# Inverses of the delta rule among the last projections, scans among the steps of attention

## What is computed

```python
mod = jax.nn.silu(c) @ lp['w_mod'] + lp['b_mod']           # 24 pieces of 256 columns, for x and for ctx
h = _rms(x, lp['norm1']) * (1 + sc1) + sh1                 # 512 tokens; hc: 256 context tokens alike
z = h @ lp['w_in']                                         # f, aq, ak, av, dqkv, dz, gates
dqkv = jax.nn.silu(_dwconv(dqkv, lp['conv_w']))            # then l2 norm of q and k
# delta rule, per direction, chunk of 64 and head:
tmat = triangular_solve(eye + lmat, eye)                   # "inverse"
def step(S, inp):                                          # "scan", chunk after chunk
    v_new = u_i - w_i @ S
    o = (q_i * exp(g_i)) @ S + qk_i @ v_new
    S = S * exp(g_last) + (k_i * exp(g_last - g_i)).T @ v_new
# attention of 8 heads in 4 blocks of 128 queries over 768 keys
p = softmax(q @ k.T * scale);  o = p @ v
cat = concatenate([fourier(f), o_att, rms(o_dn) * silu(dz)])
x = x + g1 * (cat @ w_out)
```

## Time and profile before

| | us |
|---|---|
| median of three runs | 3356.98 |
| the profiled execution | 3348.67 |
| its span | 3346.8 |
| TensorE busy in the span | 3172.3 (95%) |
| VectorE busy | 1792.9 (54%) |
| ScalarE busy | 1110.7 (33%) |
| GpSimd busy | 65.1 (2%) |

### The profile page before, as it was taken

How to read it: one execution, slowest core, us unless ns; L and a number is a source line. 1 busy time by engine, 2 the same in 40 slices (tenths; PEclk the granted TensorE clock), 3 DMA queues, 4 the chain that set the end, 5 groups by cost and what they waited for, 6 DMA issues and landing times.

```text
span 3346.8 us, 42586 instructions
## 1 busy us (share of the span) xinstructions
PE 3172.3 (95%) x17664; PEld 2506.3 (75%) x17664; DVE 1792.9 (54%) x2536; ACT 1110.7 (33%) x1566; POOL 65.1 (2%) x95
## 2 busy tenths in 40 slices
PE   6886879989999999999999999999999999999997
PEld 3654774578888888876688888888887767888886
DVE  4444565353435434487865434654345877643446
ACT  3331115342323223324443222432224244432233
POOL 0000320000000000000000000000000000000000
PEclk8887998999999999999999999999999999999999
DMA  6231000023322232321122322233222212222222
GB/s 240 82 118 64 4 32 1 26 76 101 96 94 100 96 100 92 96 94 50 62 96 99 96 95 92 96 109 96 99 87 91 91 45 84 93 101 95 95 91 73
DMA packets 81935, 288.18 MB, mean 86 GB/s; under 512 B 9552, under 2 KB 11344, under 8 KB 81360
## 3 DMA queue, kind: packets, MB, share of 16 engines
q1 hardware_dynamic: 81744, 285.46, 25.3%
HBM read 283.33 MB, written 2.10 MB: 85 GB/s over the span
## 4 chain that ended last, share of the span: by engine, by line
PE 85%; DVE 4%; issue 2%; ACT 1%; DMA 1%; POOL 0%; DVEq 0%; ACTq 0%; POOLq 0%
PE PS L1308 74%; PE PS L1390 2%; PE PS L1616 1%; PE PS L1560 1%; PE PS L1580 1%; PE PS L1618 1%; PE PS L1568 1%; PE PS L1637 1%; PE PS L1626 1%; DMA MW<-in_w_mod 1%; DVE SM L2239 0%; PE PS L1599 0%; PE PS L1350 0%; ACT SPL L1667 0%; DVE GC L2407 0%
## 5 line engine op out<-in xcount | busy, mean ns | idle before, releaser
L1308 PE MATMUL PS<-HS,SPL 128*128 128x512 f32 (+1 forms) x7752 | 1802.3, 393 | 10.0 <-DVE HS L1991 7.3
L1308 PEld LDWEIGHTS PS<-HS,SPL 128*128 128x128 f32 (+1 forms) x7752 | 1454.9, 188 | 328.7 <-issue 20.0
L1943 DVE TENSOR_TENSOR SPL<-RAW,SPL 128x1024 fp32r<-128x1024 f32 (+1 forms) x491 | 584.1, 1193 | 722.4 <-ACT SPL L1667 718.8
L1667 ACT ACTIVATE SPL<-RAW 128x1024 fp32r<-128x1024 f32 (+1 forms) x491 | 502.9, 1028 | 871.0 <-PE PS L1308 870.7
L1308 PE MATMUL PS<-FF,SPL 128*128 128x512 f32 x2880 | 654.6, 390 | 0.0
L1308 PEld LDWEIGHTS PS<-FF,SPL 128*128 128x128 f32 x2880 | 541.0, 188 | 111.8
L2324 DVE SCALAR_TENSOR_TENSOR CA<-AP__150,CW,CA 128x512 f32<-128x512 f32 x240 | 180.1, 750 | 6.2
L1844 ACT ACTIVATE FF<-TMP 128x512 fp32r<-128x512 f32 x88 | 55.7, 633 | 235.1 <-DVE TMP L2294 235.1
L1838 ACT ACTIVATE SA<-SA 128x512 f32<-128x512 f32 x88 | 55.5, 633 | 191.7 <-DVE SA L2284 191.7
L2284 DVE TENSOR_TENSOR SA<-PS,R 128x512 f32<-128x512 f32 x88 | 60.5, 691 | 98.8 <-PE PS L1308 98.5
L2239 DVE TENSOR_REDUCE SM<-PS 128x1 f32<-128x768 f32 (+2 forms) x96 | 61.8, 644 | 82.5 <-PE PS L1561 45.1
(11 more groups left out here) (290 smaller groups left out, 2309.9 us busy)
## 6 DMA issues: line engine op xcount, KB each, us to landing
RAW<-in_w_ff_in SPq DMA_DIRECT2D x176, 512.0 KB, 3.6
RAW<-in_w_in SPq DMA_DIRECT2D x88, 512.0 KB, 3.6
RAW<-in_w_ff_out SPq DMA_DIRECT2D x80, 512.0 KB, 3.5
RAW<-in_w_ff SPq DMA_DIRECT2D x64, 512.0 KB, 3.6
MW<-in_w_mod SPq DMA_DIRECT2D x48, 512.0 KB, 4.8
RAW<-in_w_out SPq DMA_DIRECT2D x24, 512.0 KB, 3.6
RAW<-in_w_ple_gate SPq DMA_DIRECT2D x16, 512.0 KB, 3.6
RAW<-in_w_ff_out SPq DMA_DIRECT2D x16, 256.0 KB, 2.6
```

Of the source, the lines that this page charges most:

```text
L1308: m = pe.matmul(o, w[x][:, k, rows], r.T[:, r.k0 + k, y, 0:r.cols], start=r.start and k == 0 and (x, y) == (0, 0), stop=r.stop and k == r. ...
L1667: a.activation(SPL[:, s, 0, 0:n], RAW[:, s, 0:n], AF.Copy).then_inc(w_hi, 1)
L1943: v.tensor_tensor(SPL[:, s, 1, 0:n], RAW[:, s, 0:n], SPL[:, s, 0, 0:n], ALU.subtract).then_inc(w_lo, 1)
```

## The change

- Stage 1: `modulate` of a pair is written after the products of the next pair, the first split stands ahead of the third pair, and SyncE asks for the first four weight pieces right behind the first eight modulation pieces.
- Stage 2: `mods_apart` gives one modulation piece at every second call of `passed` in place of four at a time. The two blocks of a `conv3` run together (`together`, two buffers `CV2`).
- The inverses are put in a list `streams` and start when keys and values are there. During the last three projections `fine` cuts a weight piece in portions of two k-tiles (6 matmuls), and after each `tick` advances the streams by 2 x `pace` steps. The projections have banks 0 to 3, the streams and norms 4 to 7. The product for `PQK` is a step of its own (`inv_pq`).
- The scans are in `streams` as well; in attention each `tick` advances three streams, twice or three times in a step u. The streams have banks 6 and 7 there.
- Attention: steps go through four blocks of queries of two heads at once; `att_values` takes 128 queries of two heads every second step (128 columns in place of 512), its result goes to `AQ`, and `att_split` writes the parts at the end. The product by the reciprocal moves from VectorE to ScalarE.
- Tiles have new places. The inverses' tiles lie over `XT`, so x is loaded again (2 MB) ahead of the residual. `RT2` is gone, `RT` is kept and loaded early.

```diff
     behind, aside, soon, rate = [], [], [], [1]
+    streams, pace, fine = [], [0], [8]
...
+            for _ in range(pace[0]):
+                if streams:
+                    x = streams.pop(0)
+                    if next(x, None) is not None:
+                        streams.append(x)
 
...
+    apart, n_passed = [], [0]
+
     def passed():
+        n_passed[0] += 1
+        if apart and n_passed[0] % 2 == 0 and next(apart[0], None) is None:
+            apart.pop()
...
+                    for at in range(0, n, fine[0]):
+                        r = Rec()
+                        r.p, r.T, r.cols, r.use, r.i, r.k0, r.at, r.ncol = p, T, cols, us[i], i, a + at, at, ncol
+                        r.n = min(fine[0], n - at)
+                        r.opens, r.start = x == 0 and i == 0 and at == 0, a + at == 0
+                        r.stop = a + at + r.n == nk
...
+    def mods_apart(js):
+        for j in js:
+            while not room(1):
+                yield 1
+            u = single()
+            for a in range(0, 8, 4):
+                r = Rec()
+                r.p, r.use, r.k0 = mod_piece(W["w_mod"][j][:, a:a + 4, :]), u, a
+                r.used = u.mark if a else count(w_used)
+                emit("mod_mm", r)
+                if a:
+                    mod_rows(j, u)
+                yield 1
...
+    for k in range(5):
         if k == 2:
             emit("split_first", None)
+        if k < 4:
+            mod(k)
+            mod(4 + k)
+        else:
...
+        if k:
+            i = 2 * k - 2
+            gain(8, "n1", i, 2, [mod_mark[k - 1], mod_mark[3 + k]])
+            hx_ready += modulate(HS, (i, i + 1), lambda j: XT[:, j, :], lambda j: SCG[:, j, 0:1],
+                                 lambda j: MOD[:, j, 0:1], R[:, :], 512, [m_r])
...
+    ev_marks, qk_done = {}, {}
+    apart.append(mods_apart(range(8, 24)))
...
+    m_msk = load("msk", MSK[:, :, :, :], D["c_levels"], hc_last[0])
...
-        while starting or len(held) > 4:
+        while starting or not room(2):
...
-        J.u4 = single() if q < 2 else None
         emit("inv_mm2", J)
...
+        give(J.u3)
+        J.kept = give(J.u2)
         if q < 2:
-            pq_ready[dd, q] = give(J.u4)
-        J.kept = J.u4.rel if q < 2 else J.u2.rel
+            while not room(1):
+                yield 1
+            J.u4 = single()
+            emit("inv_pq", J)
+            J.kept = pq_ready[dd, q] = give(J.u4)
+        emit("inv_masks", J)
...
+    jobs = [(dd, q) for n in range(3) for dd, q in ((0, (2, 0, 1)[n]), (1, (2, 1, 0)[n]))]
+    streams.extend(chained(a, jobs[a::3]) for a in range(3))
+
+
+    side_pairs[0], side[0] = (2, 3), (4, 5, 6, 7)
+    pairs[0], fine[0], rate[0], pace[0] = (0, 1), 2, 2, 2
+    for j, T, blk, key in ((1, AQ, 0, "q"), (2, AQ, 2, "q"), (7, DZ, 0, "z")):
+        hs_last = dense(W["w_in"][j], 8, HS, None, evac_to(T, blk, key))
+    while later or apart or soon:
+        passed()
+        tick()
+    fine[0] = 8
+
+
...
+            while (dd, c // 4) not in y_ready or not room(1):
...
+    scans = [scan(i, i // 2, i % 2) for i in range(4)]
+    streams.extend(scans)
...
-    m_dd = load("dftd", DFD[:, :], D["c_dftd"], *gdn_end)
-    m_df = load("dft", DFT[:, :, :, :], D["c_dft"], *gdn_end)
-    m_rt2 = load("rot2", RT2[:, :, :], D["c_rot"], *gdn_end)
+    side_pairs[0], side[0] = (3,), (6, 7)
+    while "k" not in qk_done or "v" not in qk_done or held & {0, 1, 2, 3, 4, 5}:
+        tick()
...
+    units = [(2 * p + h, qb) for p in range(4) for qb in range(4) for h in range(2)]
...
-        s.uses, s.waits = us, [qk_done["q", s.h // 2], kd_ready[-1]] if s.qb == 0 else []
-        s.pb_after = pb_after[u % 4]
+        s.uses, s.waits = us, [qk_done["q", s.h // 2], kd_ready[-1]] if u % 8 == 0 else []
+        s.pb_after, s.by = pb_after[u % 4], "scalar"
...
-    def att_values(h0, mark):
+    def att_values(u, mark):
         s = Rec()
-        s.h0, s.use, s.mark, s.after = h0, take(6 + (h0 // 2) % 2), mark, dn_ready + gdn_end
-        s.hi = count(s_ahi)
+        s.u, s.p, s.qb, s.use, s.mark = u, units[u][0] // 2, units[u][1], take(5), mark
...
+        pt_after[(u // 2) % 2] = [s.use.mark]
+        att_done[s.p] = give(s.use)
...
+    pace[0] = 3
     for u in range(36):
...
             m = att_turn(u - 3)
...
             tick()
-        else:
...
+    for p in range(4):
+        r = Rec()
+        r.p, r.waits = p, [att_done[p], *pb_after[:4]]
+        r.hi, cat_ready[p] = count(s_ahi), count(s_alo)
+        emit("att_split", r)
...
+    m_x2 = load("x2", XT[:, :, :], D["xT"], *y_ready.values())
...
+        for p in pieces[:4]:
+            fetch(p)
...
+            v.reciprocal(s.stat[:, 1:2], s.stat[:, 1:2]).then_inc(s_rs, 1)
+            if s.by == "vector":
+                v.wait_ge(*s.inv)
...
+        def scale_rows(s):
+            if s.by == "scalar":
+                a.wait_ge(*s.inv)
+                a.activation(s.row[:, 0:s.n], s.row[:, 0:s.n], AF.Copy, scale=s.stat[:, 1:2]).then_inc(s_p, 1)
```

More of the change, by code:

```diff
@@ L228, in give, with pair @@
         return us[0].rel
-    pairs = [(0, 1, 2, 3)]
-    def pair():
-        k = next(k for k in range(turn[0], turn[0] + 8)
-                 if k % 4 in pairs[0] and not {2 * (k % 4), 2 * (k % 4) + 1} & held)
+    pairs, side_pairs, side = [(0, 1, 2, 3)], [(0, 1, 2, 3)], [tuple(range(8))]
+    def pair(which=None):
+        which = which or pairs[0]
+        k = next(k for k in range(turn[0], turn[0] + 8) if k % 4 in which and not {2 * (k % 4), 2 * (k % 4) + 1} & held)
         turn[0] = k + 1
@@ L238, in single, with room, pair_room @@
     def single():
-        k = next(k for k in range(turn[1], turn[1] + 8) if k % 8 not in held)
+        k = next(k for k in range(turn[1], turn[1] + 8) if k % 8 in side[0] and k % 8 not in held)
         turn[1] = k + 1
         return take(k % 8)
+    def room(n):
+        return len([b for b in side[0] if b not in held]) >= n
+    def pair_room():
+        return any(not {2 * k, 2 * k + 1} & held for k in side_pairs[0])
     slot_end, slot_turn = [None] * 3, [0]
@@ L581, in head_norm @@
         yield 1
-        r.uses = pair() if n > 512 else (single(),)
+        while not (pair_room() if n > 512 else room(1)):
+            yield 1
+        r.uses = pair(side_pairs[0]) if n > 512 else (single(),)
         emit("head_mm", r)
@@ L689, in inverse @@
             yield 1
-            while len(held) > 6:
+            while not room(2 if lv < 5 else 1):
                 yield 1
@@ L699, in inverse @@
         y_ready[dd, q] = my
-    def alternate(streams):
-        live = list(streams)
-        while live:
-            live = [s for s in live if next(s, None) is not None]
     def chained(a, jobs):
@@ L863, in build @@
         r = Rec()
-        r.cb, r.use, r.waits, r.after = cb, single(), [f_in, m_df], dn_ready
+        r.cb, r.use, r.waits = cb, single(), [f_in, m_df]
         r.hi = count(s_ahi)
```

314 lines of the change are left out of this document (162 added, 152 removed).

## The result

The changed kernel takes 3380.24 us (median of 5 runs, 3379.79 to 3391.83), the kernel before 3356.98 (3349.24 to 3363.15). The ratio is 1.0081, with a 95% interval of 1.0057 to 1.0105: 0.8% slower, where I had forecast 3261 us and given "slower" 4 in 100. The profiled execution has a span of 3378.4 us, 31.6 more than before.

The account below looks back on a forecast made before the run. TensorE, busy for 95% of the span, was taken as the bound, leaving 134 us idle and the clock to win. Terms -6, -28, -46, -12 sum to -92: 3257 us, 3261 as a median; 8-in-10 range 3220 to 3308.

Parts of the forecast that it names:

- Part 1: The start, to 55.4 us: splits moved ahead of the third pair let the first large product come earlier, -6 us.
- Part 2: Projections with context, 55 to 212 us: fewer modulation waits, less idle time and a better clock, -28 us.
- two blocks side by side hide some of it, 5 stay: Projections with context: of 10.0 us idle at convolution norms and the like, 5 remain.
- Part 3: Last projections with the inverses laid between: 202 us for 247.6, with 30 us idle, -46 us.
- Part 4: Attention with the scans laid between its steps: 155 us in place of 167.4, -12 us.
- three head pairs in a row: Scans in attention: on two banks the third pair waits for VectorE, adding 1.7 us a round, 9.8 each.
- nine steps at 3.2, 29: End of attention: the last nine steps carry no scan and take 3.2 us each, 29 us together.
- The scaling: Attention: scaling on ScalarE is free while nothing else is late, otherwise +0.3 us a step, +10 us in the bounds.
- Part 5: The rest, Fourier part and all behind it, with the second load of x covered: 0 us.
- (b): Rival: head pairs stop for banks, rounds of 12.5 us, projections with inverses idle for 50 us; 3306 us, chance 0.17.
- (c): Rival: each stream step holds TensorE for a 1.1 us trip to VectorE or ScalarE; 3369 to 3375 us, chance 0.05.
- The signs that I set: Expected: `MW` waits under 6 us, clock 0.95 or more; refuting: small-product VectorE waits above 60 us, rounds over 12 us.

Follow-up runs that it names:

- e11_conv_apart: e7_read_pace2 with the convolution blocks for q and k one after another instead of side by side: 3303.82 us.
- e1_apart: The changed kernel with nothing laid between: inverses and scans together on eight banks after the last projections, then attention alone: 3398.26 us.
- e2_inv: The changed kernel with inverses still between the projections, but all scans ahead of attention on eight banks: 3403.96 us.
- e8_apart_read: e1_apart with attention's transposes ahead of the scores, values behind them and read by VectorE, and one repeated product dropped: 3329.33 us.
- e6_inv_read: e2_inv with attention's transposes ahead of the scores, values behind them and read by VectorE, and one repeated product dropped: 3331.71 us.
- e5_read: The changed kernel with attention's transposes ahead of the scores, values behind them and read by VectorE, one repeated product dropped: 3357.46 us.
- e7_read_pace2: e5_read with two steps of the scans in a row between attention's steps in place of three: 3306.19 us.
- e13_apart_read_vec: e8_apart_read with attention's scaling back on VectorE instead of ScalarE: 3312.16 us.
- e9_pace2: The changed kernel with two steps of the scans in a row in place of three, attention's order as it was: 3340.16 us.

## Why the prediction was wrong, step by step

- **Part 1, forecast -6: right.** The first large product is at 50.7 us, before at 55.4, so -4.8.
- **Part 2, forecast -28: wrong in size.** The last product with context ends 8.7 us earlier (194.3 against 203.0), and 4.8 of these are part 1's, so some 4 to 6 us are left for this part. The waits for `MW` went nearly as said, from 16.9 us to 5.3 (I had said 3). Idle time is 20.8 us, not 8. The failed term is "two blocks side by side hide some of it, 5 stay". VectorE in the changed kernel:

```profile
152.37 4.97 DVE L2163 RECIPROCAL XD<-XD 128x770 f32<-128x770 f32 x1 [0.91 <-ACT XD L1824]
157.25 0.90 DVE L2157 TENSOR_SCALAR XD<-PS 128x770 f32<-128x770 f32 x1
158.07 1.21 DVE L2047 TENSOR_TENSOR SPL<-RAW,SPL 128x1024 fp32r<-128x1024 f32 x1
159.19 1.02 DVE L2172 SCALAR_TENSOR_TENSOR KC<-CV,XD 128x512 f32<-128x512 f32 x2
160.13 4.96 DVE L2163 RECIPROCAL XD<-XD 128x770 f32<-128x770 f32 x1
```

Side by side puts both reciprocals of 5 us in a row, and the turns of k on TensorE stop for them (4.0 and 3.3 us), with the projections queued behind. The clock, of which I expected 10 us back, is 0.89 (before 0.88). One after another, the stops only move (e11_conv_apart), and 2 us come back.
- **Part 3, forecast -46, bounds -76 to -6: in the bounds, for another reason.** From 201.5 to the last inverse at 425.3 it is 223.8 us for 247.6: -24. TensorE's busy time was 187 us against my 172, idle 37 against 30; 6 of the 187 are `k_both` and the first scores, which I had counted in part 4. But the gain isn't the inverses' place: without it (e1_apart against e2_inv, e8_apart_read against e6_inv_read) the last scan ends just as early. My reading is that before, scans and inverses hid each other's answers; with the inverses between projections, the scans stand alone (419 to 463 us in e2_inv). I had counted the cover gained and not the cover lost. Of the waits for the second set of modulation pieces, 15.0 us in the earlier trace rows, none is left where the inverses lie between; it is 6.0 in e1_apart and 8.1 in e8_apart_read.
- **Part 4, forecast -12, bounds -26 to +21: this is the step that failed.** 236.5 us in place of 155. Two terms of it. First, "three head pairs in a row ... the third stops until VectorE has read the first: I add 1.7 a round". I saw the mechanism and mis-sized it: the stops are 3.05 us in a round at full clock (562.9 to 574.3: 0.97, 0.56, 1.15, 0.37), where a round takes 11.4 us; with the stage's clock of 0.77, which I had not priced, it is 13.6 in the mean. Price by e5_read against e7_read_pace2: 51 us, with the spreading of the scans in it. Second, "nine steps at 3.2, 29". From the last scan to the last values it took 74.2 us. Nine was a wrong count to begin with: nine scores stood there, but thirteen sets of transposes and eight products with values, by my estimate from rows of this stage at full clock some 38 us (1.5 for scores, 0.8 for transposes, 1.5 for values, 3 for the outputs between). And a step at 3.2 is read from the earlier trace rows, where transposes stand ahead of scores and values come once in eight steps; I moved the duration to a written order that is another. Price of the written order: 23 us in this kernel, 70 where attention is alone. With both costs taken away (e7_read_pace2) it is 155.4 us from the first scores and 159.2 from `k_both`, with which my 155 begins. So near a number is partly luck: the scans are spread over more steps there, and my count of the last steps was some 9 us short.
- **The scaling, +0.3 a step at most: wrong.** I compared ScalarE's sum (2.84 us a step) with TensorE's and called it free. It is 0.5 us a step where attention is alone (e13_apart_read_vec), since the copy for the values has to pass it. With the scans beside it, it is a gain of 6 to 26. The Trainium skill (Perfetto Trace Analysis, Optimizing Scalar/DVE Operations) says that handing work to ScalarE may make sense if VectorE is saturated. The runs agree with the loss where VectorE has little to do (14.1 of 50 us in e8_apart_read). But the gain came with VectorE busy in 91 of 156 us (e7_read_pace2) and 72 of 163 (the changed kernel), far from saturated; here the measurement decides.
- **Part 5, the rest at 0: right.** The second load of x cost nothing: from the last values to `w_out` it is 19.9 us, before 19.6.
- **The rivals.** (b) named the bank and rounds of 12.5 us, and priced them for the full clock. (c), 3369 to 3375, is nearest in time to 3380, but a trip for every step is not what happened: in e7_read_pace2 the same steps stand between attention's, and only 2.5 us of stops are left. What decided for the scans was how many of them stand in a row against how many banks they have. The loop in attention's own order stood in none of the rivals. The Trainium skill (Perfetto Trace Analysis, Optimizing Tensor Performance, Matmuls) asks that independent groups rotate through banks, so that the reading of one lies beside the next. The runs agree, and give a price for one group too many: at most 51 us for three on two banks, and at most 88 for two on one.
- **The signs that I set.** Rounds over 12 us: seen. Waits for VectorE at the small products over 60 us in sum: seen, some 28 at the scans and 39 at the inverses and turns. Waits for `MW` under 6 us: seen. Clock of 0.95 or more from 60 us: not seen.

## What to carry to other kernels

A duration per step is that of its written order: before moving it to another order, follow one step backwards through the in-order queues and ask whether an engine waits for an answer to its own last instruction. When work is laid between, count how many pieces in a row use the same buffers, and give them no more in a row than they have buffers; with one piece more the changed kernel is slower than the one before, with one less (e9_pace2) it is faster. Look also at what is left over behind the last piece, for it finds no cover. And price a stop on TensorE with the clock that goes with it: in e1_apart a stop of 2.28 us stood in 13.8 us, and the low clock took some 5.7 of them.

## What the runs showed of the hardware that I had not expected

- TensorE can stay at its lower clock though it is busy most of the time and its stops are short: busy in 43.16 of 50 us with a stop of 2.28 in each 13.8, clock 0.50 (e1_apart, 550 to 600 us). At a busy time of 41.27 of 50 the clock was 0.90 in e6_inv_read. The busy share alone does not tell the clock; part of the share is the low clock itself, since the same work lasts twice as long.
- Rounds of scans between steps of attention, with stops of up to 1.0 us, went with a clock of 0.59 at 455 to 515 us of the changed kernel, and with stops of up to 1.1 us with 0.97 at 515 to 580 us. (Up to 485 us the rounds are without outputs; 485 to 500 us, with them, still has 0.51.) What makes the difference was not tried.
- The reciprocal of 128x770 on VectorE took 4.97 us, an operation with a scalar on that size (157.25 in the rows above) 0.90.
- A scaling of 0.92 us on ScalarE, done on VectorE instead, changed the time by +26, +6 or -17 us, by what stood beside it (0.62 us on VectorE in the earlier trace rows).
